# Convolution taps in one operation over both requests, and one tap more moved from TensorE to VectorE

## What is computed

```python
CONV_WIDTH = 31

def depthwise_conv(x, w, b):
    pad = w.shape[0] // 2
    y = lax.conv_general_dilated(
        x, w[:, None, :].astype(x.dtype), window_strides=(1,), padding=[(pad, pad)],
        dimension_numbers=('NWC', 'WIO', 'NWC'), feature_group_count=x.shape[-1])
    return y + b

def conformer_conv(x, w_pw1, b_pw1, w_dw, b_dw, g_n, b_n, w_pw2, b_pw2):
    h = x @ w_pw1 + b_pw1
    a, gate = jnp.split(h, 2, axis=-1)
    h = a * jax.nn.sigmoid(gate)
    h = depthwise_conv(h, w_dw, b_dw)
    h = jax.nn.silu(layer_norm(h, g_n, b_n))
    return h @ w_pw2 + b_pw2
...
for i in range(DEPTH):          # DEPTH = 2: layer 0 convolution, layer 1 attention
    ...
    x = layer_norm(DEEPNORM_ALPHA * x + mix, ln_mix_g[i], ln_mix_b[i])
    f = conv_ffn(x, ffn_w_up[i], ffn_w_dw[i], ffn_b_dw[i], ffn_w_down[i])
    x = layer_norm(DEEPNORM_ALPHA * x + f, ln_ffn_g[i], ln_ffn_b[i])
```

## Time and profile before

| | |
|---|---|
| median of 3 runs | 3003.24 us (3001.82 to 3005.05) |
| the profiled execution | 3003.5 us |
| its span, first to last instruction | 3001.1 us |
| PE busy | 2876.8 us, 96% |
| DVE busy | 1640.7 us, 55% |
| GpSimd busy | 911.8 us, 30% |
| ScalarE busy | 749.3 us, 25% |
| mean granted clock of TensorE | 0.984 of full speed |

### The profile page before, as it was taken

How to read it: one execution, slowest core, us unless ns; L and a number is a source line. 1 busy time by engine, 2 the same in 40 slices (tenths; PEclk the granted TensorE clock), 3 DMA queues, 4 the chain that set the end, 5 groups by cost and what they waited for, 6 DMA issues and landing times.

```text
span 3001.1 us, 36000 instructions
## 1 busy us (share of the span) xinstructions
PE 2876.8 (96%) x14070; PEld 2347.4 (78%) x14070; DVE 1640.7 (55%) x2612; ACT 749.3 (25%) x1717; POOL 911.8 (30%) x798
## 2 busy tenths in 40 slices
PE   8999959999999999999899899899999999999995
PEld 7888848788888888888788544487888888888884
DVE  3699974744444444444730599727444444444457
ACT  3212343221111111222111466502222111111131
POOL 3354502232233233232132333323223223223323
PEclk9999979999999999999999899999999999999998
DMA  4000003111111111111221000021111111111111
GB/s 131 29 18 25 28 1 119 29 43 31 40 43 39 33 43 43 36 43 36 71 78 32 22 1 1 23 94 36 43 36 40 31 43 43 36 36 43 43 36 70
DMA packets 158644, 124.65 MB, mean 42 GB/s; under 512 B 27905, under 2 KB 135801, under 8 KB 158488
## 3 DMA queue, kind: packets, MB, share of 16 engines
q1 hardware_dynamic: 149640, 96.83, 11.3%
q10 hardware_dynamic: 8848, 25.69, 2.3%
HBM read 112.01 MB, written 10.49 MB: 41 GB/s over the span
## 4 chain that ended last, share of the span: by engine, by line
PE 86%; DVE 9%; ACT 3%; issue 1%; DMA 0%; POOL 0%; POOLq 0%; ACTq 0%; SPq 0%; DVEq 0%
PE bank L588 26%; PE bank L593 26%; PE bank L591 26%; PE bank L953 3%; PE bank L929 2%; DVE conv_acc L1293 2%; PE bank L944 1%; DVE stats L1223 1%; DVE y L1241 1%; DVE x_lo L1249 1%; ACT y L1094 1%; DVE y L1236 1%; DVE y L1451 1%; PE bank L618 1%; ACT probs L1187 1%
## 5 line engine op out<-in xcount | busy, mean ns | idle before, releaser
L588 PE MATMUL bank<-x_hi,w_hi 128*128 128x512 f32 (+1 forms) x2688 | 957.2, 356 | 3.8 <-DVE x_lo L1249 1.6
L591 PE MATMUL bank<-x_lo,w_hi 128*128 128x512 f32 (+1 forms) x2688 | 953.4, 355 | 0.0
L593 PE MATMUL bank<-x_hi,w_lo 128*128 128x512 f32 (+1 forms) x2688 | 953.3, 355 | 0.0
L514 POOL CAST w_hi<-raw_pieces 128x512 fp32r<-128x512 f32 x348 | 329.9, 948 | 1802.9 <-issue 1363.8
L588 PEld LDWEIGHTS bank<-x_hi,w_hi 128*128 128x128 f32 x2688 | 509.5, 190 | 79.0 <-POOL w_lo L518 6.3
L591 PEld LDWEIGHTS bank<-x_lo,w_hi 128*128 128x128 f32 x2688 | 509.5, 190 | 70.6
L593 PEld LDWEIGHTS bank<-x_hi,w_lo 128*128 128x128 f32 x2688 | 509.1, 189 | 70.8
L518 POOL TENSOR_TENSOR w_lo<-raw_pieces,w_hi 128x512 fp32r<-128x512 f32 x348 | 472.2, 1357 | 27.9
L1451 DVE TENSOR_TENSOR y<-y,bank 128x512 f32<-128x512 f32 x440 | 296.2, 684 | 200.5 <-PE bank L593 198.5
L1412 DVE SCALAR_TENSOR_TENSOR gate_conv<-bank,ffn_conv_table,gate_conv 128x510 f32<-128x510 f32 x132 | 86.2, 653 | 373.5 <-ACT up_conv L1125 371.5
L1293 DVE SCALAR_TENSOR_TENSOR conv_acc<-glu,conv_table,conv_acc 128x1024 f32<-128x1024 f32 (+1 forms) x310 | 257.6, 906 | 35.4 <-ACT conv_acc L1034 35.4
(11 more groups left out here) (144 smaller groups left out, 3765.5 us busy)
## 6 DMA issues: line engine op xcount, KB each, us to landing
raw_pieces<-in_ffn_w_up_dram SPq DMA_DIRECT2D x168, 256.0 KB, 2.9
raw_pieces<-in_ffn_w_down_dram SPq DMA_DIRECT2D x84, 256.0 KB, 2.6
raw_pieces<-in_conv_w_pw_dram SPq DMA_DIRECT2D x48, 256.0 KB, 2.7
y<-in_x_prompt_dram ACTq DMA_DIRECT2D x16, 512.0 KB, 6.8
residual_dram<-y ACTq DMA_DIRECT2D x10, 512.0 KB, 2.6
y<-residual_dram ACTq DMA_DIRECT2D x10, 512.0 KB, 10.7
out_dram<-y SPq DMA_DIRECT2D x10, 512.0 KB, 2.6
raw_pieces<-in_attn_w_q_dram SPq DMA_DIRECT2D x32, 128.0 KB, 2.4
```

Source lines behind the costliest of these rows:

```text
L514: pool.tensor_copy(WH[:, p % RING, :], raw[:, p % RAW, :]).then_inc(piece_hi, 1)
L588: mm = pe.matmul(out, left[0], right[0], start=first, stop=False)
L591: pe.matmul(out, left[0], right[1], start=False, stop=False)
L593: return pe.matmul(out, left[1], right[0], start=False, stop=last)
```

## The change

TensorE's share of the taps goes from nine to eight on every tile, and from 22 to 24 on the last. DVE so has 23 taps on tiles 0 to 6, and 7 instead of 9 on tile 7. Of these all but the last are one operation each, of 1295 columns, over the prompt, the 15 columns between and the sample; what is computed in the 15 columns is not used. The last tap stays two operations, since `conv` has no gap. Each operation now waits for the one just before it. The tables and the diagonals take the new numbers of taps.

```diff
-    PE_TAPS = 9
-    MORE_TAPS = 13
+    PE_TAPS = 8
+    MORE_TAPS = 16
...
                 dve.wait_ge(acc_ready, i * 6 + 3 * c + 3)
-                for k in range(taps):
-                    last = k == taps - 1
-                    for c0, n, a0 in ((0, S0, 0), (S0, S1, S0 + PAD)):
-                        if k > 0:
-
-                            dve.wait_ge(vec_step, vs.now() - (0 if last and c0 else 1))
-                        ins = dve.scalar_tensor_tensor(
-                            out=conv[:, bass.ds(i * 2 + c, 1), c0:c0 + n] if last else acc[:, c, a0:a0 + n],
-                            in0=glu[:, c, a0 + k:a0 + k + n], scalar=tap(k), in1=acc[:, c, a0:a0 + n],
-                            op0=ALU.mult, op1=ALU.add)
-                        if not last:
-                            ins.then_inc(vec_step, vs.one())
+                n = S0 + PAD + S1
+                for k in range(taps - 1):
+                    if k > 0:
+                        dve.wait_ge(vec_step, vs.now())
+                    dve.scalar_tensor_tensor(out=acc[:, c, :], in0=glu[:, c, k:k + n], scalar=tap(k),
+                                             in1=acc[:, c, :], op0=ALU.mult, op1=ALU.add
+                                             ).then_inc(vec_step, vs.one())
                     if k == 3:
                         between()
+                dve.wait_ge(vec_step, vs.now())
+                k = taps - 1
+                for c0, n, a0 in ((0, S0, 0), (S0, S1, S0 + PAD)):
+                    ins = dve.scalar_tensor_tensor(
+                        out=conv[:, bass.ds(i * 2 + c, 1), c0:c0 + n], in0=glu[:, c, a0 + k:a0 + k + n],
+                        scalar=tap(k), in1=acc[:, c, a0:a0 + n], op0=ALU.mult, op1=ALU.add)
                 ins.then_inc(conv_done, 1)
...
-            vs.rounds(dve, KT // 2 - 1, conv_round, 2 * 2 * (V_TAPS - 1))
+            vs.rounds(dve, KT // 2 - 1, conv_round, 2 * (V_TAPS - 1))
```

## The result

The changed kernel takes 3021.57 us (median, 3021.18 to 3023.66), the kernel before, timed with it, 3002.53 (2999.76 to 3005.05). The ratio is 1.0063, 95% interval 1.005 to 1.0077. The forecast was 3020.5 us with a chance of 0.79 on slower. The profiled execution has a span of 3019.6 us, 18.5 more than before, at a mean granted clock of 0.98.

What follows compares the result with a forecast made beforehand. PE bounds the convolution stage to about 312 us, then DVE; after the change DVE limits at once. 14.7 + 2.3 + 3.5 - 3.15 = 17.3 us on 3003.5, less 0.26, gives 3020.5 us; 8-in-10 range 3002 to 3030.

Steps and rivals of the forecast that it cites:

- The pitch of merged operations: DVE's merged convolution taps: 1.56 us each, starting 1.60 us apart in straight code, 1.70 in the loop; a pair had 1.59.
- The hand-over to GpSimd: Between DVE's serial taps GpSimd takes turns at SBUF: 4.34 us a piece, adding 4.56 a tile straight, 3.76 in the loop.
- The beat: DVE's time per channel tile in the loop: 40.31 + 3.76 + 2.03 = 46.10 us, against 41.5 for PE.
- Tile 7: Last channel tile: PE's two more taps add 3.49 us, DVE's fewer taps save 3.15, PE's slow clock adds 2.3.
- Rival 3: Convolution stage: PE keeps the limit because one operation pays one fixed cost, 0.2 us a tap; 2992.3 us, chance 0.06.
- The start: DVE's first tap of tile 0 moves from 96.12 to 94.37 us, as PE has one tap of 1.745 us less.
- The later stages: Stages behind the convolution have the same instructions and only move.
- PE's idle time before tile 7: PE idles 7.1 us before its taps of tile 7, where it was about 1.4 before.
- a slow restart: PE at 1.2 GHz after idling: 2.3 us (0 to 3.0) at tile 7, covered by its wait in earlier tiles.
- rival 2: GpSimd uses the gaps between DVE's taps without costing DVE anything: 7.7 us less, 2995.5 us, chance 0.11.

Runs made afterwards that it cites:

- Experiment 3: The changed kernel with DVE's loop over tiles 1 to 4 written out, so waits are constants: 3015.18 us, ratio 1.0044 to the kernel before.
- Experiment 4: The changed kernel with GpSimd writing zeros instead of reading and splitting weight pieces 8 to 47: 2997.23 us, ratio 0.9984 to the kernel before.
- experiment 5: The changed kernel with DVE's loop written out and GpSimd writing zeros instead of splitting those weights: 2993.79 us, ratio 0.9969 to the kernel before.
- experiment 1: The kernel before with only TensorE's share changed (8 taps, 24 on tile 7), DVE's taps still overlapping pairs: 3012.31 us, ratio 1.0029.
- experiment 7: The kernel before, but on tile 7 DVE sums its taps without waiting for TensorE's sum; TensorE 26 taps, DVE 5: 2993.18 us, ratio 0.9974.
- experiment 2: The changed kernel with TensorE's old share (9 taps, 22 on tile 7), DVE's taps merged: 3011.86 us, ratio 1.0035 to the kernel before.
- experiment 6: The kernel before with one operation per tile, the prompt's of tap 17, waiting for the operation just ahead: 3012.0 us, ratio 1.0029.
- experiment 8: The kernel before with DVE's tile 7 sum not waiting for TensorE's, TensorE 24 taps there and DVE 7: 2998.02 us, ratio 0.9985.

## Why the prediction was right, step by step

- **The pitch of merged operations.** Predicted 1.56 us of duration, starts 1.60 apart in straight code and 1.70 in the loop. Measured 1.57, 1.60 and 1.71. Experiment 3 shows the loop's share at work, 1.7 us a tile.
- **The hand-over to GpSimd.** Predicted 4.34 us a piece where DVE gets two operations done; measured 4.36. Taps of tile 0: predicted 42.77, measured 139.21 - 96.36 = 42.85. Tile 1 in the loop: 44.07 and 44.33. Experiment 4 takes the reads away and finds 0.93 us a piece, for 0.94. This is the largest term, and the step that was argued from the least: one cast and one subtraction in the earlier trace rows. The prediction says that GpSimd is shut out in the kernel before; it leaves unsaid that turns were taken there too where a tile's taps begin on its last pieces. DVE's first eight operations take 6.46 us in tile 0 and 8.47 in tile 5. The sum doesn't use this.
- **The beat.** Predicted 46.10, measured 46.3 in the loop. PE's own 41.5 is shown by experiment 5, and by the first beat of 1 and 4 (41.69).
- **Tile 7.** Predicted + 3.49 for PE's two taps and + 2.3 for the clock: from PE's first tap to DVE's first 45.30 us pass (373.95 to 419.25), 39.52 before, so + 5.78. DVE's end: - 3.12, predicted - 3.15.
- **Rival 3 and the fixed cost.** Two operations that overlap had already hidden it. With neither reads nor loop (experiment 5) the 18 merged operations in the middle of a tile take 28.82 us, which is 1.60 apart, where a pair had 1.59. A saved fixed cost would show there. The 0.2 us a tap of that rival are in the durations (1.76 against 1.57) and not in the pitch.

Three things were off, and two of them cancelled:

- **The start.** DVE's first tap was to move from 96.12 to 94.37 and moved to 96.36. Starts of all traces with nine taps: 96.12, 96.44, 98.13, 98.17, 99.02; with eight: 96.24 to 96.36, five times. So the trace of before was an early one, by about 2 us, of a start that varies by 3. The traces show where: TensorE's first products of the projection, of 128 x 512, take 0.39 to 0.40 us each in the two earliest traces of nine taps (before, experiment 7), and at least the first six take some 0.63 us in the other eight. Before, then the changed kernel:

```profile
17.19 0.39 PE L591 MATMUL bank<-x_lo,w_hi 128*128 128x512 f32 x1
```

```profile
17.86 0.63 PE L591 MATMUL bank<-x_lo,w_hi 128*128 128x512 f32 x1
```

That is the time of a product at a granted clock of 0.51 elsewhere (373.95 to 379), although the clock column reads 1.00 here. By the transposes of the tables, at 42.05 and 44.01 us, all of the 2 us is there. Against an ordinary start with nine taps (98.13 in experiment 2) the saved tap gives its 1.77 us, as predicted. By the start, 0.8 of beats and 0.2 of tile 5, PE's taps of tile 7 came 17.7 us later and not 14.7, and DVE's last tap ends at 430.6 and not at about 427.
- **The later stages.** They were to move unchanged. From DVE's last tap to the end of the span 2590.9 us passed before (3001.1 - 410.18) and 2589.1 after, 1.9 less. 1.3 of it are one stretch, from the first feed-forward block to the second, which lasts 1486.3 us in the traces of before and of experiment 1, and 1484.4 to 1485.0 in the other eight, those of experiments 6 and 7 among them, which have the old pairs. So it isn't the change that gave it back. It is TensorE's clock once more. Behind the same pause of 2.29 us in the attention, four products take 3.59 us in the trace of before (3.60 in that of experiment 1), and 1.90 in the changed kernel:

```profile
1933.33 3.59 PE L953 MATMUL bank<-probs_T,v 128*64 128x512 f32 x4 [2.29 <-ACT probs_T L1199]
```

```profile
1953.41 1.90 PE L953 MATMUL bank<-probs_T,v 128*64 128x512 f32 x4 [2.29 <-ACT probs_T L1199]
```

The granted clock is 0.57 from 1933 to 1937 in the trace of before, and 1.00 at the same place in the changed one. Why it fell in two traces of ten is open. The - 1.9 and + 3.0 leave the 1.2 by which the span of 18.5 exceeds the forecast's 17.3.
- **PE's idle time before tile 7** was to be 7.1 us and was 4.2. I had counted half clock only behind that idle time, and taken a slow restart in the loop as covered. It did come there (the 7 us at 232), so PE's projections got longer, its waits in the loop shorter (14.8 us in five, for 4.6 each), and so was its idle time here. On the path nothing changed, as DVE set the end.

The forecast had the right sign and mechanism. How much hung on one step is seen in rival 2 (no hindrance): experiment 4, where GpSimd reads nothing, comes to 2997.2 us, near that rival's 2995.5. Whether GpSimd's reads cost DVE time decided between slower and faster. That the measured 3021.6 lies within 1.1 us of the forecast is in part luck, by the two errors that cancelled.

The 19 us by parts: the share alone + 9.8 (experiment 1), the merge on top of it + 9.3 (3012.3 to 3021.6), and the merge at the old share + 9.3 as well (experiment 2). These go by the 3002.5 of the result. By the ratio of the executions timed together experiment 1 is 8.7 us slower (5.4 to 12.0) and experiment 2 10.5 (6.6 to 14.7), so the parts are not known to better than 3 to 4 us. From the other end: the reads of GpSimd cost the changed kernel 24.3 us, the loop 6.4, or 3.4 where there are no reads. Without both it takes 2993.8 us.

## What to carry to other kernels

Before serial operations with two SBUF inputs replace overlapping ones on DVE, count what GpSimd has to read from SBUF in that time: the overlapping chain mostly shut it out, the serial one shares with it, and each 128 x 512 piece split cost DVE 0.9 to 1.4 us. Count the pitch of operations and not their duration, since two that overlap may already have the pace of one. And look for the pause that an engine makes for a hand-over at the end of a stage: taking it out gave 9.0 us by the medians, of which 6.7 are seen in the rows of the stage. The balance within the stage gave 8.7 at its best.

## What the runs showed of the hardware

- A cast that waits for SBUF beside overlapping DVE operations can wait until their chain ends. The longest wait is in experiment 1, 18.75 us, through more than 20 operations:

```profile
L514 POOL CAST w_hi<-raw_pieces x24: 611/808/18754, 119.1 to 367.6; 128x512 fp32r<-128x512 f32 x24
```

The Trainium skill ("SBUF — State Buffer", Who interferes with whom) has the two exclude each other, and the one that issues first go first; that the lock lasts for the whole instruction it says of VectorE's 2-port modes. The rows add that the next DVE operation, which issues after the waiting GpSimd instruction, still goes ahead of it where it overlaps the last. In the changed kernel, where each waits for the one just ahead, the two take turns and the trace agrees.

- One operation that waits for the one just ahead is enough for GpSimd to get in (experiment 6), at times even none that is to be seen (experiment 1, 308 us), for a reason that is open. From there on the two engines alternate until its pieces are done.
- A GpSimd write of 128 x 512 takes 0.52 us and leaves DVE's operation beside it at 1.57 (experiment 4).
- PE's granted clock was at half, 1.2 GHz, behind a pause of 4.2 us (the changed kernel, 372 to 379 us), and at full over pauses of 0.20 to 1.07 us between transposes (experiment 7). The length of the pause alone doesn't decide: behind 1.49 us 16 transposes took 2.07 us in experiment 7 and 3.22 in experiment 8, and behind 2.3 us in the attention four products took 1.90 us in eight traces and 3.6 in two.
